# Hybrid block, attention stage: p scaled on GpSimd, transposed once in fp32, split while leaving PSUM

## The reference

```python
for i in range(S // Q_BLOCK):                       # 8 blocks of 128 queries
    lo, hi = i * Q_BLOCK, (i + 1) * Q_BLOCK
    s = jnp.einsum('bhqd,bhkd->bhqk', q[:, :, lo:hi], k[:, :, :hi]).astype(jnp.float32) * scale
    s = s + F[:, :, lo:hi, None] - F[:, :, None, :hi]
    mask = (lo + jnp.arange(Q_BLOCK))[:, None] >= jnp.arange(hi)[None, :]
    s = jnp.where(mask, s, -jnp.inf)
    p = jax.nn.softmax(s, axis=-1).astype(v.dtype)
    outs.append(jnp.einsum('bhqk,bhkd->bhqd', p, v[:, :, :hi]))
```

## Time and profile before

| what | value |
|---|---|
| three runs | 1545.2, 1547.29, 1549.36 us, median 1547.29 us |
| the profiled execution, its span | 1547.3 us |
| attention stage, from the first exp to the last values | about 112 to 437 us |
| PE busy over the whole span | 1452.8 us, 94% |
| DVE, ACT, POOL busy over the span | 482.1, 482.1 and 414.5 us |
| p_low on DVE (L1170), 64 instructions | 72.3 us |
| transposes on PE (L1560), 576 instructions | 41.8 and 39.1 us of overlapping busy time |

### The profile page before, as it was taken

The page is one execution under the profiler, slowest core; times in us unless marked ns, Lnnn a source line. Parts: engine busy times, 40 slices in busy tenths (PEclk is TensorE's granted clock), DMA queues, the critical chain, the costliest instruction groups (busy, mean ns, idle before and its releaser), DMA issues.

```text
span 1547.3 us, 18728 instructions
## 1 busy us (share of the span) xinstructions
PE 1452.8 (94%) x6864; PEld 1200.1 (78%) x6864; DVE 482.1 (31%) x711; ACT 482.1 (31%) x770; POOL 414.5 (27%) x221
## 2 busy tenths in 40 slices
PE   4989889888986999999999999999999999999997
PEld 4977777777764888888878888888888888888885
DVE  4526666666566211111362211111111111113113
ACT  4445565656542111112342111111111112223322
POOL 1131211212132222223451222121212223444443
PEclk9999999999996999999999999999999999999999
DMA  5211031111132212324451111111111121243522
GB/s 173 48 30 23 22 50 21 42 27 40 36 107 61 43 42 50 45 54 135 151 182 50 42 54 41 54 41 54 48 47 54 41 68 68 95 149 116 171 93 96
DMA packets 113339, 106.80 MB, mean 69 GB/s; under 512 B 6576, under 2 KB 89008, under 8 KB 113264
## 3 DMA queue, kind: packets, MB, share of 16 engines
...
...
## 4 chain that ended last, share of the span: by engine, by line
PE 68%; DVE 3%; ACT 1%; issue 0%; DMA 0%; SPq 0%; POOL 0%; POOLq 0%; DVEq 0%; ACTq 0%
PE ps L1435 46%; PE ps L1696 21%; DVE pool_lo L1247 0%; DVE win L1263 0%; DVE head_tmp L1271 0%; PE ps L1745 0%; PE ps L1575 0%; DMA pscale<-in_pool_scale 0%; DVE y_out L1053 0%; DVE y L1313 0%; PE ps L1560 0%; DVE pool L1272 0%; DVE h_lo L1319 0%; DVE win L1262 0%; DMA at_d<-at_st 0%
## 5 line engine op out<-in xcount | busy, mean ns | idle before, releaser
L503 POOL TENSOR_TENSOR w_lo<-w_raw,w_hi 128x1024 fp32r<-128x1024 f32 (+1 forms) x141 | 338.6, 2403 | 964.9 <-ACT w_hi L649 964.9
L1435 PE MATMUL ps<-h_lo,w_hi 128*128 128x512 f32 x1152 | 296.5, 398 | 0.0
L1435 PE MATMUL ps<-h_hi,w_hi 128*128 128x512 f32 x1152 | 292.1, 395 | 3.2 <-DVE h_lo L1319 2.4
L1435 PE MATMUL ps<-h_hi,w_lo 128*128 128x512 f32 x1152 | 286.9, 390 | 0.0
L1435 PEld LDWEIGHTS ps<-h_lo,w_hi 128*128 128x128 f32 x1152 | 219.6, 192 | 45.5
L1435 PEld LDWEIGHTS ps<-h_hi,w_hi 128*128 128x128 f32 x1152 | 215.8, 190 | 48.4 <-DVE h_lo L1319 2.6
L1435 PEld LDWEIGHTS ps<-h_hi,w_lo 128*128 128x128 f32 x1152 | 215.4, 188 | 44.6
L649 ACT ACTIVATE w_hi<-w_raw 128x1024 fp32r<-128x1024 f32 (+1 forms) x141 | 145.2, 1033 | 280.6 <-PE ps L1435 279.6
L1696 PE MATMUL ps<-w_lo,lg_hi 128*128 128x512 f32 x344 | 108.5, 396 | 0.0
L1696 PE MATMUL ps<-w_hi,lg_lo 128*128 128x512 f32 x344 | 108.5, 396 | 0.0
L1696 PE MATMUL ps<-w_hi,lg_hi 128*128 128x512 f32 x344 | 108.5, 396 | 0.0
...
## 6 DMA issues: line engine op xcount, KB each, us to landing
...
```

Of the source, the lines that this page charges most:

```text
L503: g.tensor_tensor(lo[:, 0:width], w_raw[c % 2][:, 0:width], hi[:, 0:width].bitcast(f32), ALU.subtract).then_inc(s_wlo, 1)
L1435: ins = mm(bank, stats[i], movs[i], start=first and i == 0, stop=last and i == n - 1)
```

## The change

p_raw is now scaled in place by POOL (`scale_p`, a tensor_tensor with the broadcast reciprocal), two steps ahead. `p_high`, `p_low` and their four buffers go. PE transposes the fp32 tiles of p_raw once, against the fp32 identity, and the rounds take banks 4 and 5 in turn. ACT copies a round to pt_hi (rounding to fp32r), and DVE then takes the same PSUM bank minus pt_hi into pt_lo. `pt_hi` and `pt_lo` become two buffers each, one for blocks 0 to 3 and one for blocks 4 to 7. `softmax_exp` of step s + 2 writes the buffer that step s is transposed from, so it now waits for the transposes of step s (`s_th`). POOL's other work is placed between the scalings.

```diff
--- before.py
+++ after.py
@@ -177,10 +177,8 @@
         q_raw = place("q_raw", [P, S])
         k_raw = place("k_raw", [P, S])
         p_raw = [place(f"p_raw{i}", [P, S]) for i in range(2)]
-        p_hi = [place(f"p_hi{i}", [P, S], f32r) for i in range(2)]
-        p_lo = [place(f"p_lo{i}", [P, S], f32r) for i in range(2)]
-        pt_hi = place("pt_hi", [P, NT, HALF], f32r)
-        pt_lo = place("pt_lo", [P, NT, HALF], f32r)
+        pt_hi = [place(f"pt_hi{i}", [P, 4 * (i + 1), HALF], f32r) for i in range(2)]
+        pt_lo = [place(f"pt_lo{i}", [P, 4 * (i + 1), HALF], f32r) for i in range(2)]
         pv_tmp = place("pv_tmp", [DH, HALF])
 
         at[0] = phase
...
@@ -565,20 +563,42 @@
             w_low(3)
             wait(pool, s_wlo, 4)
 
+            def scale_p(p, s):
+
+                n = ((s % 8) + 1) * P
+                wait(pool, s_rc, 16 * p + s + 1)
+                g.tensor_tensor(p_raw[s % 2][:, 0:n], p_raw[s % 2][:, 0:n],
+                                rowinv[s % 2][:].to_broadcast([P, n]), ALU.mult).then_inc(s_pn, 1)
+
             def attention(p, last):
-                stack_low(p, 1)
-                v_low(p, 1)
+                for s in range(16):
+                    if s == 0:
+                        wait(pool, s_pn, 16 * p + 2)
+                        stack_low(p, 1)
+                    if s < 14 or not last:
+                        scale_p(p, s + 2)
+                    if s == 1:
+                        v_low(p, 1)
+                    if last:
+                        if s in (5, 9, 15):
+                            w_low(C_GATE + 1 + (5, 9, 15).index(s))
+                        continue
+                    if s == 5:
+                        w_low(4, 4 * p, 512)
+                    if s == 10:
+                        w_low(5, 4 * p, 512)
+                    if s == 11:
+                        wait(pool, s_pn, 16 * p + 14)
+                        stack_low(p + 1, 0)
+                    if s == 13:
+                        v_low(p + 1, 0)
                 if not last:
-                    w_low(4, 4 * p, 512)
-                    w_low(5, 4 * p, 512)
-                    stack_low(p + 1, 0)
-                    v_low(p + 1, 0)
                     w_low(6, 4 * p)
                     w_low(7, 4 * p)
                     wait(pool, s_wlo, 4 * p + 8)
-                else:
-                    for c in range(C_GATE + 1, C_GATE + 4):
-                        w_low(c)
+
+            scale_p(0, 0)
+            scale_p(0, 1)
 
             attention(0, False)
             with pool.Fori(1, 3) as p:
@@ -735,30 +755,22 @@
 
                 n = ((s % 8) + 1) * P
                 wait(act, s_mx, 16 * p + s + 1)
-                wait(act, s_plo, 16 * p + s - 1)
+                wait(act, s_th, RPAIR * p + RSUM[s - 1] if s > 0 else RPAIR * p - ROUNDS[15])
                 wait(act, s_rc, 16 * p + s - 1)
                 b = 1024 * (s % 2)
                 a.activation(p_raw[s % 2][:, 0:n], ps_flat[:, b:b + n], ACT.Exp, bias=negmax[s % 2][:],
                              accum_out=rowsum[s % 2][:]).then_inc(s_exp, 1)
 
-            def p_high(p, s):
-                n = ((s % 8) + 1) * P
-                wait(act, s_rc, 16 * p + s + 1)
-                wait(act, s_exp, 16 * p + s + 1)
-                wait(act, s_th, RPAIR * p + RSUM[s - 1] if s > 0 else RPAIR * p - ROUNDS[15])
-                a.activation(p_hi[s % 2][:, 0:n], p_raw[s % 2][:, 0:n], ACT.Copy,
-                             scale=rowinv[s % 2][:]).then_inc(s_phi, 1)
-
             def evac_t(p, s):
 
                 i = s % 8
                 if i % 4 == 0:
-                    wait(act, s_pv, 4 * p + s // 4)
+                    wait(act, s_pv, 4 * p + s // 4 - 1)
                 for r in range(ROUNDS[s]):
                     n = min(4, i + 1 - 4 * r)
                     wait(act, s_th, RPAIR * p + RSUM[s] + r + 1)
-                    a.activation(pt_hi[:, 4 * r:4 * r + n, (i % 4) * P:(i % 4) * P + P],
-                                 ps[:, 4, 0:n * P].rearrange("p (k n) -> p k n", n=P),
+                    a.activation(pt_hi[i // 4][:, 4 * r:4 * r + n, (i % 4) * P:(i % 4) * P + P],
+                                 ps[:, 4 + (RSUM[s] + r) % 2, 0:n * P].rearrange("p (k n) -> p k n", n=P),
                                  ACT.Copy).then_inc(s_evh, 1)
 
             def evac_pv(p, g4):
...
@@ -796,8 +807,6 @@
                 for s in range(16):
                     if s == 0:
                         stack_high(p, 1)
-                    if s < 15 or not last:
-                        p_high(p, s + 1)
                     if s < 14 or not last:
                         softmax_exp(p, s + 2)
                     unit, _, until = (FILL_LAST if last else FILL).get(s, (0, 0, 0))
@@ -1159,27 +1168,20 @@
 
             def row_inv(p, s):
                 wait(dve, s_exp, 16 * p + s + 1)
-                wait(dve, s_phi, 16 * p + s - 1)
+                wait(dve, s_pn, 16 * p + s - 1)
                 v.reciprocal(rowinv[s % 2][:], rowsum[s % 2][:]).then_inc(s_rc, 1)
-
-            def p_low(p, s):
-                n = ((s % 8) + 1) * P
-                wait(dve, s_phi, 16 * p + s + 1)
-                wait(dve, s_rc, 16 * p + s + 1)
-                wait(dve, s_tl, RPAIR * p + RSUM[s - 1] if s > 0 else RPAIR * p - ROUNDS[15])
-                v.scalar_tensor_tensor(p_lo[s % 2][:, 0:n], p_raw[s % 2][:, 0:n], rowinv[s % 2][:],
-                                       p_hi[s % 2][:, 0:n].bitcast(f32), ALU.mult,
-                                       ALU.subtract).then_inc(s_plo, 1)
 
             def evac_t(p, s):
                 i = s % 8
                 if i % 4 == 0:
-                    wait(dve, s_pv, 4 * p + s // 4)
+                    wait(dve, s_pv, 4 * p + s // 4 - 1)
                 for r in range(ROUNDS[s]):
                     n = min(4, i + 1 - 4 * r)
-                    wait(dve, s_tl, RPAIR * p + RSUM[s] + r + 1)
-                    v.tensor_copy(pt_lo[:, 4 * r:4 * r + n, (i % 4) * P:(i % 4) * P + P],
-                                  ps[:, 5, 0:n * P].rearrange("p (k n) -> p k n", n=P)).then_inc(s_evl, 1)
+                    wait(dve, s_evh, RPAIR * p + RSUM[s] + r + 1)
+                    cut = (slice(None), slice(4 * r, 4 * r + n), slice((i % 4) * P, (i % 4) * P + P))
+                    v.tensor_tensor(pt_lo[i // 4][cut],
+                                    ps[:, 4 + (RSUM[s] + r) % 2, 0:n * P].rearrange("p (k n) -> p k n", n=P),
+                                    pt_hi[i // 4][cut].bitcast(f32), ALU.subtract).then_inc(s_evl, 1)
 
             def evac_pv(p, g4):
 
...
@@ -1203,8 +1204,6 @@
                     if s == 0:
                         stack_q(p, 1)
                         stack_k(p, 1)
-                    if s < 15 or not last:
-                        p_low(p, s + 1)
                     if s < 14 or not last:
                         row_inv(p, s + 2)
                     evac_t(p, s)
@@ -1550,16 +1549,15 @@
 
             def transposes(p, s, r):
 
-                i = s % 8
-                n = min(4, i + 1 - 4 * r)
-                for src, ready, free, done, bank in ((p_hi, s_phi, s_evh, s_th, 4), (p_lo, s_plo, s_evl, s_tl, 5)):
-                    if r == 0:
-                        wait(pe, ready, 16 * p + s + 1)
-                    wait(pe, free, RPAIR * p + RSUM[s] + r)
-                    for k in range(n):
-                        ins = nc.tensor.transpose(ps[:, bank, P * k:P * k + P].bitcast(f32r),
-                                                  src[s % 2][:, (4 * r + k) * P:(4 * r + k + 1) * P], ident_r[:])
-                    ins.then_inc(done, 1)
+                n = min(4, s % 8 + 1 - 4 * r)
+                if r == 0:
+                    wait(pe, s_pn, 16 * p + s + 1)
+                wait(pe, s_evl, RPAIR * p + RSUM[s] + r - 1)
+                bank = 4 + (RSUM[s] + r) % 2
+                for k in range(n):
+                    ins = nc.tensor.transpose(ps[:, bank, P * k:P * k + P],
+                                              p_raw[s % 2][:, (4 * r + k) * P:(4 * r + k + 1) * P], ident[:])
+                ins.then_inc(s_th, 1)
 
             def values(p, s):
 
@@ -1569,7 +1567,7 @@
                 wait(pe, s_evl, RPAIR * p + RSUM[s + 1])
                 wait(pe, s_pvev, 4 * p + s // 4)
                 nk = 4 * g + 4
-                for x_, pt in enumerate((pt_hi, pt_lo)):
+                for x_, pt in enumerate((pt_hi[g], pt_lo[g])):
                     for k in range(nk):
                         q0 = max(0, k - 4 * g) * P
                         ins = mm(ps[:, 6, q0:HALF], vs[e][:, k, :], pt[:, k, q0:HALF],
```

6 lines of the change are left out of this document (2 added, 4 removed).

## The result

The changed kernel takes 1557.8 us (median of 4 runs, 1557.1 to 1563.5) against 1547.7 us before (4 runs, 1545.2 to 1549.4): a ratio of 1.0069, 95% interval 1.0054 to 1.0084. It is 0.7% slower. The span of its profiled execution is 1556.0 us, 8.7 more than before.

The account below looks back on a forecast made before the run. PE was taken to set the end, losing 38.2 us idle in attention plus time at half clock. Terms -13 + 22 - 9 + 0.3 + 0 + 3 = +3.3 on 1547.3, rounded up to 1551 us; range 1538 to 1565.

Parts of the forecast that it names:

- the side that had the highest chance: Whole kernel: slower than before by more than about 0.3%, given a chance of 0.44.
- the likeliest case: Whole kernel: gains and losses nearly cancel, 1551 us with its own range 1544 to 1557; chance 43%.
- Transposes: PE work in attention: 576 at 0.073 us become 288 at 0.100 us, -13 us.
- Waits ahead of values: PE before `values` in steps 3, 7, 11, 15: longer idle behind exp, copies and subtraction, +22 us in four pairs.
- The waits inside steps 4 to 7 and 12 to 15: PE between transpose rounds: three waits of 1.0 to 1.1 us replace short bank waits, 0 (±1 per pair).
- Heads: Start of each pair: PE waits 2.0 us for exp(2) and scale(2) instead of 4.31, -9 us in four pairs.
- Clock: PE's half-clock stretches in attention: some 15 losing about 1.3 us each, 19 against 16 before, +3 us.
- The sum: Whole kernel: all terms together +3.3 us on 1547.3, rounded up to 1551 us.
- Subtraction 0.68 whatever POOL does: DVE's new subtraction, one operand from PSUM: 0.68 us even beside a busy POOL.
- GpSimd hidden except at the head: POOL's scaling costs PE some time only at pair heads; elsewhere, at the tightest place, 2 us to spare.
- the clock falls with every long wait: Slow-side rival in attention: about 24 half-clock stretches of 1.3 us, +15 us, 1562 us; chance 19%.

Follow-up runs that it names:

- c_transpose_twice: Changed kernel with four p_raw buffers (pt_hi and pt_lo single again), every transpose issued twice, against that kernel's 1500.2 us: 1528.2 us.
- d_subtract_first: Changed kernel with ACT's projection copy and copies of step s ahead of exp(s + 2), and DVE's subtraction ahead of row_inv(s + 2): 1505.0 us.
- a_proj_first: Changed kernel with ACT's copy of a finished projection moved ahead of exp(s + 2), the exp still ahead of the copies of step s: 1534.1 us.
- c_four_scale_dve: Changed kernel with four p_raw buffers and the scaling on DVE behind the subtraction instead of on GpSimd: 1535.1 us.

## Why the prediction was right, and which step failed

The time lies in the range and on the side that had the highest chance, 0.44. It is above the likeliest case's own range (1544 to 1557) by less than 1 us. By its steps:

- **Transposes, -13, "certain to within a microsecond or two".** This term was too small. The price after the change was right, 90 to 97 ns by c_transpose_twice. The price before was not: 73 ns is the distance inside one group of four, and over all 576 the trace shows 94 ns. Their time on PE fell from 54.1 to 30.3 us, -24.
- **Waits ahead of values, +22.** Measured 36.9 - 13.9 = +23.0. For step 7 of the second pair 2.65 us stand where 2.6 were worked out, and for step 3 1.95 where 2.05 were. The size was right for the changed kernel; the cause was told by half. I took the copies on ACT behind the exp for the whole chain. d_subtract_first shows row_inv on DVE as a second way from exp to subtraction: ACT's order alone left 34.9 us ahead of `values`, with DVE's order as well 21.8 are left.
- **The waits inside steps 4 to 7 and 12 to 15, "I take 0 (between -1 and +1 per pair)".** This step failed: measured 22.4 - 9.1 = +13.3 us, 3.3 per pair. I followed the banks 4 and 5 only. The projection copy was in my chain for `values`, as work ahead of the copies, but I did not ask who waits for it itself: it empties the bank that the next fill needs. The wait that I did work out, the next step's transposes for the subtraction, some 3 us per pair, is 2.9 us in all four. 19.5 of the 22.4 us are the wait for the projection copy, after steps 5, 8, 10 and 12, and a_proj_first takes them away with 24 us.
- **Heads, -9.** Measured 6.9 - 14.8 = -7.9, with 0.63 us for exp and 1.46 for scale(2) at the second pair, where 0.5 and 1.5 were priced. The 384 columns took 0.83 us, not 1.0.
- **Clock, +3.** Right in size: 19.5 - 16.7 = +2.8 us by the two sums above, from ten stretches (two of them 6.8 us long) where 15 of 3.4 us were expected.
- **The sum.** The three kinds of wait give 23.0 + 13.3 - 7.9 = +28.4 us, where +13 was expected, and the transposes -24, where -13 was. With the clock's 2.8 that is +7.4 of the stage's +9.4; the other 2 us are not accounted for. The sum came within 7 us because two terms were wrong by 13.3 and by about 11 us the opposite way. That part is luck.
- **Subtraction 0.68 whatever POOL does.** 690 ns as the mean of 48, with a maximum of 693, though 34 of the 48 lie on an instruction of POOL. This is also what the Trainium skill says (SBUF - State Buffer, "Who interferes with whom").
- **GpSimd hidden except at the head.** Right: POOL's scaling ends waits of PE for 4.5 us, all at the heads. The Trainium skill (GPSIMD Engine Reference, its opening) calls GpSimd the wrong choice for ordinary elementwise arithmetic. That holds for the duration (896 columns take 1681 ns, on DVE 677) and not for the time of this kernel: on DVE, in the order tried, the scaling costs 17 to 35 us more.

Of the rivals, "the clock falls with every long wait" got the nearest number (1562) for another reason; there were fewer such stretches, not more.

Open: c_four_scale_dve's loop is argued from the order and the waits, and no run takes a single link of it away. Why one wait of 1.9 us is followed by the lower clock and another is not, no run tells. Four buffers with the copies and the subtraction both first were not tried. Nor was the kernel before given orders of this kind, so how much of the 53 or 58 us belongs to these transposes, and how much a better order would have given without them, stays open.
